# A two-layer hybrid encoder on one core: the query projection is fed with tokens that are not yet normalised, and the convolution's normalisation is put elsewhere

## What is computed

```python
for l in range(DEPTH):
    z = _rms(h, norm1_g[l]) @ w_in[l]
    ya = _attention_group(...)      # 8 heads, windowed
    yr = _rwkv_group(...)           # 4 heads, a recurrent state
    yc = _conv_group(...)           # 31 taps, then layernorm and silu
    h = h + jnp.concatenate([ya, yr, yc], axis=-1) @ w_out[l]
    h = h + _peer(_rms(h, norm2_g[l]), peer_wq[l], peer_keys[l], peer_u[l], peer_v[l])

def _rms(x, g):
    return x * lax.rsqrt(jnp.mean(x * x, axis=-1, keepdims=True) + NORM_EPS) * g

# _peer: q = xn @ wq; s = q . keys; top 16 of each half; top 16 of their 256 sums;
# gate = softmax(the 16 sums); hid = gelu(xn . u[row]); out = sum(gate * hid * v[row])
```

## Time and profile before

| | |
|---|---|
| time, median of 3 runs | 1869.92 us (1866.32 to 1876.38) |
| the profiled execution's own time | 1865.88 us |
| its span in the profile | 1864.0 us |
| TensorE busy | 1783.0 us (96%) |
| VectorE busy | 1452.3 us (78%) |
| ScalarE, GpSimd busy | 837.5 us, 875.0 us |

### The profile page before, as it was taken

One profiled execution on the slowest core, in us unless ns is written; L12 is line 12 of the kernel. 1 busy time (PEld: TensorE's weight loads), 2 busy tenths in 40 slices (PEclk: granted clock), 3 DMA queues, 4 the chain that ended last, 5 costly groups with the idle time before them and its releaser, 6 DMA issues.

```text
span 1864.0 us, 39016 instructions
## 1 busy us (share of the span) xinstructions
PE 1783.0 (96%) x14384; PEld 1735.8 (93%) x14384; DVE 1452.3 (78%) x3027; ACT 837.5 (45%) x1771; POOL 875.0 (47%) x635
## 2 busy tenths in 40 slices
PE   9978899999999899999999788999999999999999
PEld 8966899999999899999989768999999999999998
DVE  2686558895499889999946755688644998999997
ACT  6523441211476545555546225412114776555543
POOL 4895560234143447676437964602341333554540
PEclk9979899999999999999999878999999999999999
DMA  5400345899899899999944002568998997999995
GB/s 197 136 2 2 104 157 192 304 402 391 340 349 339 299 345 415 420 419 412 392 141 155 2 2 91 173 205 315 375 409 304 328 339 279 381 388 391 387 385 188
DMA packets 138648, 505.84 MB, mean 271 GB/s; under 512 B 15392, under 2 KB 15520, under 8 KB 138272
## 3 DMA queue, kind: packets, MB, share of 16 engines
q1 hardware_dynamic: 87840, 319.68, 46.2%
q0 software_dynamic: 50688, 184.57, 26.0%
HBM read 503.14 MB, written 1.05 MB: 270 GB/s over the span
## 4 chain that ended last, share of the span: by engine, by line
PE 69%; DVE 20%; DMA 5%; issue 4%; ACT 2%; SPq 0%; ACTq 0%; POOL 0%; DVEq 0%; POOLq 0%
PE ps L1100 69%; DMA w<-v_c 5%; DVE arena L2164 3%; DVE onehots_i L2096 2%; DVE rows_w L1942 2%; DVE w_lo L2148 1%; DVE x_hi L2140 1%; DVE arena L2117 1%; DVE rows_x L1942 1%; ACT w_hi L789 1%; DVE x L1662 1%; DVE x_lo L1655 1%; DVE arena L1677 1%; DVE arena L1707 1%; DVE onehots_j L1650 0%
## 5 line engine op out<-in xcount | busy, mean ns | idle before, releaser
L1100 PE MATMUL ps<-x_hi,w_hi 128*128 128x352 f32 (+2 forms) x2544 | 721.8, 342 | 20.6 <-DVE x_lo L1655 10.9
L1100 PE MATMUL ps<-x_hi,w_lo 128*128 128x176 f32 (+2 forms) x2544 | 646.8, 254 | 0.0
L1100 PE MATMUL ps<-x,w 128*128 128x176 f32 x4096 | 627.8, 313 | 0.0
L1100 PEld LDWEIGHTS ps<-x,w 128*128 128x128 f32 x4096 | 612.5, 190 | 0.6 <-issue 0.2
L1100 PEld LDWEIGHTS ps<-x_hi,w_hi 128*128 128x128 f32 x2544 | 480.0, 189 | 35.3 <-DVE x_hi L2140 10.1
L1100 PEld LDWEIGHTS ps<-x_hi,w_lo 128*128 128x128 f32 x2544 | 485.7, 191 | 0.0
L789 ACT CAST w_hi<-w 128x1024 fp32r<-128x1024 f32 x318 | 334.2, 1051 | 318.2 <-DMA w<-v_c 234.0
L717 POOL DMA_INDIRECT arena<-v_c,sel x176 | 311.3, 1769 | 226.4 <-DVE arena L2164 199.6
L685 POOL TENSOR_TENSOR w_lo<-w,w_hi 128x1024 fp32r<-128x1024 f32 x90 | 222.4, 2485 | 211.7 <-ACT w_hi L789 211.6
L2148 DVE TENSOR_TENSOR w_lo<-w,w_hi 128x1024 fp32r<-128x1024 f32 x228 | 278.0, 1219 | 32.2 <-ACT w_hi L789 31.6
L717 POOL DMA_INDIRECT rows_w<-ur_c,sel x116 | 120.7, 1040 | 232.5 <-DVE sel L1942 222.7
(11 more groups left out here) (196 smaller groups left out, 1739.5 us busy)
## 6 DMA issues: line engine op xcount, KB each, us to landing
w<-u_c SPq DMA_DIRECT2D x256, 512.0 KB, 5.7
w<-v_c SPq DMA_DIRECT2D x256, 512.0 KB, 6.5
w<-w_c SPq DMA_DIRECT2D x84, 512.0 KB, 3.5
arena<-v_c,sel POOLq DMA_INDIRECT x176, 8.2
arena<-keys_c SPq DMA_DIRECT2D x2, 1024.0 KB, 8.3
arena<-mix_c SPq DMA_DIRECT2D x2, 964.0 KB, 8.8
rows_w<-ur_c,sel POOLq DMA_INDIRECT x116, 7.9
h<-h SPq DMA_DIRECT2D x2, 544.0 KB, 5.0
```

Source lines behind the costliest of these rows:

```text
L1100: return nc.tensor.matmul(out_, lhsT, rhs, start=start, stop=stop, skip_group_check=True)
```

## The change

The query projection multiplies tokens that lack the root-mean-square factor: `raw_high` and `raw_low` make the two halves of `h` times `norm2` chunk by chunk, as soon as `w_out`'s tile has been added, in two new buffers. `square_sums` comes behind query tile 0, ScalarE's root behind the evacuation of that tile, and the zero matmuls at this place are gone. The factor itself is turned from a row to one number per partition (`turn_scales`, behind query tile 2) and enters the softmax as the scale of the exponential. `xn` is still made, now for the `u` tiles, without high and low halves; the replicated tokens are copied from it and transposed four query tiles later than before, and `restore` is gone.

The convolution's layernorm gets new places: its first sum over channels is at place 44 of TensorE in place of 51, the second at 48 in place of 52, its VectorE steps at 33 and 36, its root on ScalarE at 14. Its bias goes into the sigmoid and into the last product, so that two VectorE instructions fall away. The last attention output is at place 51. `w_out` takes the chunks in the order 0 to 7. VectorE makes the low halves of the first three `w_out` tiles, before the first `gram` product; GpSimd begins with the fourth.

```diff
-CONV_PE = ((51, 52,),
+CONV_PE = ((44, 48,),
...
-CONV_ACT = ((18, 18,),
+CONV_ACT = ((14, 18,),
...
-CONV_DVE = ((37, 38, 38, 38,),
+CONV_DVE = ((33, 36,),
...
-CONV_ORDER = (0, 1, 2, 3, 6, 7, 4, 5)
+CONV_ORDER = tuple(range(8))
...
-                lows(l, NZ, NPROJ)
+                pool.wait_ge(s_lo, l * NPL + NZ + AHEAD)
+                lows(l, NZ + AHEAD, NPROJ)
...
+            def raw_high(l, t0, c):
+
+                act.wait_ge(s_ed, l * NOUT + c + 1)
+                nc.scalar.activation(raw_hi[:, c, t0:T], h[:, c, t0:T], ACT.Identity,
+                                     scale=vcol(l, "norm2", c)).then_inc(s_xh, 1)
...
                 x_high(l, 1, cat, L.t0, range(4))
+                act.wait_ge(s_pe, REQUESTS * l + REQUESTS - 2)
+                x_high(l, 1, cat, L.t0, (4, 5))
                 act.wait_ge(s_cat, l + 1)
                 x_high(l, 1, cat, L.t0, (6, 7))
...
                 for m in range(NOUT):
                     high(l, NZ + m + AHEAD)
                     if m:
+                        raw_high(l, L.t0, m - 1)
                         square(l, 1, m - 1)
+                raw_high(l, L.t0, NOUT - 1)
                 square(l, 1, NOUT - 1)
-                norm_scale(l, 1)
-                x_high(l, 2, xn, L.t0)
...
+                    evacuate(l, NZ + NOUT + m, pq[:, m, L.t0:T], L.nt)
                     if m == 0:
...
+                        norm_scale(l, 1)
...
-                        ins = nc.scalar.activation(gates_, gates_, ACT.Exp)
+                        ins = nc.scalar.activation(gates_, gates_, ACT.Exp, scale=scale_t[:, 2 * s:2 * s + 1])
...
-                square_sums(l, 1)
-                warm(WARM["norm"], 3)
...
+                    project(l, n, L.t0, ready=None if m else x_split(l, 2), hi=raw_hi, lo=raw_lo)
+                    if m == 0:
+                        square_sums(l, 1)
+                    if m == 2:
+                        turn_scales()
...
+            def raw_low(l, t0, c):
+
+                dve.wait_ge(s_xh, (3 * l + 2) * DC + c + 1)
+                v.scalar_tensor_tensor(raw_lo[:, c, t0:T], h[:, c, t0:T], vcol(l, "norm2", c),
+                                       raw_hi[:, c, t0:T].bitcast(F32), ALU.mult, ALU.subtract).then_inc(s_xl, 1)
...
+                for n in range(NZ, NZ + AHEAD):
+                    dve.wait_ge(s_lo, l * NPL + n)
+                    dve.wait_ge(s_hi, highs_to(l, n))
+                    v.tensor_tensor(low_of(l, n, wlo_t), low_of(l, n, wraw_t), high_of(l, n).bitcast(F32),
+                                    ALU.subtract).then_inc(s_lo, 1)
...
-                beside.rest()
+                beside()
                 pe_done()
                 pe_done()
...
-                for c in CONV_ORDER:
+                for c in range(4):
+                    x_low(l, 1, cat, xl, L.t0, c)
+                beside.rest()
+                for c in range(4, DC):
                     x_low(l, 1, cat, xl, L.t0, c)
...
+                    if m:
+                        dve.wait_ge(s_ed, l * NOUT + m)
+                        raw_low(l, L.t0, m - 1)
```

More of the change, by code:

```diff
@@ L309, in trunk @@
         zero_t = sb("zeros", P + 2)
-        arena_t = sb("arena", ARENA)
+        scale_t = sb("token_scales", 2 * NT)
+        with nc.sbuf_tensor("arena", [P, ARENA], F32) as arena_t:
+            pass
+        sb("below_raw", RAW_AT)
+        raw_lo_t = sb("raw_low", DC * T, F32R)
+        sb("between_raw", NZ * (T + 1) - DC * T)
+        raw_hi_t = sb("raw_high", DC * T, F32R)
+        sb("above_raw", ARENA - RAW_AT - NZ * (T + 1) - DC * T)
         ps = ctx.enter_context(nc.psum_tensor("ps", [P, 8, 512], F32))
@@ L894, in conv_norm @@
                 act.wait_ge(s_cs, l + 1)
[L895 removed]
+                for j in range(2):
+                    ins = nc.scalar.activation(cu[:, j, 0:T], ctmp[:, j, :], ACT.Sigmoid, bias=vcol(l, "ln_b", j))
+                ins.then_inc(s_cg, 1)
                 yield
@@ L1436, in _, with turn_scales @@
                     project(l, n, L.t0, ready=None if m else x_split(l, 1), order=CONV_ORDER)
-                square_sums(l, 1)
-                warm(WARM["norm"], 3)
+                    if m == 0:
+                        asked()
+                def turn_scales():
+                    pe.wait_ge(s_xn, (2 * l + 1) * DC + 1)
+                    for s, (t0, nt) in enumerate(L.tiles):
+                        for q in range(PACK if L.tiles[s] == PACKED else 1):
+                            r = slice(32 * q, 32 * q + 32) if L.tiles[s] == PACKED else slice(0, nt)
+                            last = mm(ps[r, 3, 2 * s:2 * s + 2], var[:, t0:t0 + r.stop - r.start], ident[:, 0:2], True, True)
+                    last.then_inc(s_rt, 1)
                 def scores(pairs):
```

99 lines of the change are left out of this document (50 added, 49 removed).

## The result

The changed kernel takes 1842.67 us (median of 4 runs, 1841.61 to 1843.52), the kernel before 1868.29 us in the same runs (1866.32 to 1876.38): a ratio of 0.9836, 95% interval 0.9801 to 0.9871. Two repeats beside the experiments gave 0.9884 (0.9856 to 0.9913) and 0.9868 (0.9839 to 0.9897). Over everything that was run, the changed kernel's median is 1843.7 us (15 runs, 1841.6 to 1853.0) and that of the kernel before 1869.8 us (72 runs, 1861.9 to 1880.2): 26 us, 24 us by the means. I had forecast 18 us (14 to 22): the right sign and the right places, with a gain that I put too small.

The account below looks back on a forecast made before the run. TensorE, busy 1783 of 1864 us, was taken to bound the kernel, with time in its waits and low clock. Norm 12.5 + convolution 6.6 - clock 1.1 = 18.0 us, from 1869.9 to 1852; range 1840 to 1861.

Parts of the forecast that it names:

- The convolution's norm: At the mixers' end: moving it into the state loop lets `w_out` begin earlier, 6.6 us over both layers.
- The sums of squares: Behind query tile 0: six instructions return to TensorE's path, costing 1.8 us per layer, 3.6 in all.
- The scales and transposes: Query stage: turned scales cost TensorE 1.1 us; the third group's transposes at layer 0's last query tile cost 0.5.
- Query tile 0 follows `w_out` without a wait: Behind `w_out`: halves arrive in time, so gaps of 8.9 and 8.8 us go, together 17.7 us.
- 3.6 us, and layer 1 gives 0.6 less: Mixers' end: `w_out` begins 3.6 us earlier in layer 0 and 3.0 us in layer 1.
- Clock, 1.1 us of loss: Start of `w_out`: TensorE's half-clock stretches, costing 3.7 us before, would change for a net loss of 1.1 us.
- The rival that the clock stays up: No half clock in `w_out` and cheap scales: gain 23.4 us, about 1846; chance 0.14 for a gain above 22.
- Low halves 0: Three low halves moved from GpSimd to VectorE before `gram`: counted 0, up to 2 us per layer if cover is thin.
- Nobody waited for them: Low halves' old place on GpSimd: its three took 6.97 us without any engine waiting.
- The late convolution: Rival: low halves push the taps by 8.1 us, TensorE stands 4.3 in layer 1; gain 10.7, about 1859; chance 0.17.
- The gain passes through: Stages after the queries: they start from the queries' end, `u` and `v` stay as long, nothing is lost.
- Slower by half clock without zeros: Rival: without zeros, half clock over 32 us of work takes all 18.0 us and 9.4 more; chance 0.04.

Follow-up runs that it names:

- fewer_zeros_in_the_tail: The changed kernel with 5 and 9 matmuls of zeros in TensorE's two pauses at the mixers' end; 1842.53 us, ratio 0.9840.
- before_again: The kernel before, unchanged, run for a second profile; ratio 1.001 to before, its profiled execution 1879.7 us.
- no_dve_lows: The changed kernel with the three low halves back on GpSimd; 1846.75 us against the whole change's 1847.41.
- early_and_fewer_zeros: The changed kernel with attention chunks' halves made earlier, `w_out`'s first two tiles sharing the wait, 5 zero matmuls ahead of the spread; 1843.75 us, ratio 0.9858.

## Why the prediction was right or wrong

The mechanisms came out as forecast, and the sum didn't: 18.0 us against 22.3 in the profiles and 24 to 26 over all runs. The step that failed is the sizing of three terms. The convolution's norm was put at 6.6 us and gave 8.9 (4.1 and 4.8, where I had 3.6 and 3.0). The sums of squares were put at 3.6 us on TensorE's path and cost 2.3 to 2.7. The scales and transposes were put at 1.6 us and cost 0.1 net. The further 2 to 4 us between profiles and medians have no experiment of their own.

- **Query tile 0 follows `w_out` without a wait**: right. The halves of chunk 7 were ready, `raw_low` of it at 217.8 us, its matmuls at 218.58.
- **"Back onto TensorE's path come the sums of squares, six instructions that take 1.8 us"**: mis-sized. They cost 1.17 to 1.37 us per layer; the row that I took counted the last instruction's length and had pauses in it. The part from `w_out`'s end to tile 1 gave 7.8 + 7.7 = 15.5 us, not 14.1.
- **Turned scales 1.1, third transposes 0.5**: mis-sized. In layer 0 the scales cost 0.63 us (226.31 to 226.94), but from tile 1 to the first `u` tile it is 59.37 us against 59.65, and 54.27 against 53.93 in layer 1: 0.1 us in all. One wait of 0.47 us (for ScalarE, at 285.98) went in layer 0; its twin in layer 1 stayed (0.46). The rest of the difference isn't traced, and the transposes were not priced by themselves.
- **"3.6 us, and layer 1 gives 0.6 less"**: the mechanism right, the size too small, above all in layer 1: 4.1 and 4.8 us from the last scores to `w_out`. In layer 0 the steps up to the recurrent norm grew by 2.7 us (I had 3.0), and the chain behind is 6.63 us long (I had 6.9). In layer 1 they grew by 2.6 us where I had 3.6 (the 3.0 and the 0.6 of the quotation), and the old chain behind them took 14.05 us (1114.11 to 1128.16), 0.6 more than the one of layer 0 on which I summed. One reason for the 2.6 is that VectorE's part of the old chain held the 1.5 us of L1714 beside GpSimd: from the last scores to the read correction it is 8.2 us (1091.42 to 1099.62) against 7.1 before, 1.1 more, while layer 0 has 7.2 against 5.6.
- **Clock, 1.1 us of loss**: about right. `w_out` is 0.5 and 0.95 us longer than before, 1.4 in all. The rival that the clock stays up did not come about with this change alone; zeros in the pauses bring it about (1.00 from the tail's pauses to `w_out`'s end in both layers of fewer_zeros_in_the_tail), and shorten the norm columns by 1.8 and 0.9 us when there are not too many.
- **Low halves 0, and the convolution isn't late**: right in this kernel's time, within the scatter. "Nobody waited for them", said of the old place on GpSimd, is wrong: L1714 in layer 1 did. The late convolution's 8.1 us of delay to the taps was an estimate, three times the 2.69 us of the earlier trace rows; no run shows it. What shows is 2.8 us of delay for 4.03 us of low halves, with 2.4 us still in hand in layer 1. So the edit has a benefit that I did not see: the old place on GpSimd collides with attention's small chain (L1714 takes 1.67 us where L1763, its place in the changed kernel, takes 0.16).
- **The gain passes through**: right within the scatter of the `u` and `v` stages, 0.9 us in sum.
- **The sum and its baseline.** By the stages it is 15.5 for `w_out`'s end to tile 1, 8.9 for the tails from the last scores, 0.8 for layer 1's mixers ahead of them and 0.9 for the `u` and `v` stages, less 1.4 for the clock in `w_out`, 1.1 for layer 0's mixers, 1.2 for the start and 0.1 for the rest of the queries: 22.3 us, where I had 18.0. Of the 4.3, 1.4 are the stretch with the sums of squares, 1.5 the scales and transposes, 2.3 the tails; the rest, which I had at 0 apart from the clock, takes 0.9 back. The execution that I summed against (1865.9 us) is shorter than most of the kernel before (median 1869.8), so the medians over all runs show 3.7 us more than the two profiles do. In before_again about half of the extra time in the mixers goes with the lower clock and half with the collision that the change takes away. How often the large collision happens isn't known, and no_dve_lows, with the low halves on GpSimd again, was no slower; what makes up the 3.7 us stays open.
- **Slower by half clock without zeros**: did not happen; the granted clock is 1.00 from 195 to 286 us and from 1120 to 1199 us, over both query stages.

## What to carry to other kernels

A projection of an RMS-normalised activation can start on unscaled tokens as soon as the residual is there, if a per-token scale can be applied later: here that is worth the norm's whole chain, less the matmuls of the sum: 7.8 and 7.7 us from `w_out`'s end to tile 1. Price a burst only after taking out the waits inside it: the row of 1.88 us stood for a cost of 1.17 to 1.37. When VectorE and GpSimd both work from SBUF, look at how their instructions interleave, not at their busy shares: making one of them earlier can cost what it gains (a start 2.4 us sooner, and in early_and_fewer_zeros a `w_out` of 26.9 us at a clock of 1.00 in place of 24.3). The VectorE instruction that grew most in proportion was a tiny one on the critical chain, up to 2.34 us for 128x4 elements in place of 0.16.
